# Fetching the value pages of a paged attention: 96 indirect DMAs on GpSimd instead of 384 register-addressed page loads

## The reference, cut to what matters

```python
gate = jnp.einsum('bqhd,bhnd->bqhn', qf, kmean)
...
top_s, top_i = lax.top_k(gate, K)
...
kg = kb[bi, hi, idx].astype(jnp.float32)
vg = vb[bi, hi, idx].astype(jnp.float32)
...
p = jax.nn.softmax(s.reshape(B, Q, H, -1), axis=-1).reshape(s.shape)
return jnp.einsum('bqhtk,bqhtkd->bqhd', p, vg)
```

## Time and profile before

| what | value |
|---|---|
| device time, median of 3 runs | 1584.08 us (1583.78 to 1584.59) |
| the profiled execution's own time | 1583.34 us |
| its span | 1581.5 us |
| PE busy | 1529.1 us, 97% |
| DVE, ACT, POOL busy | 944.3, 645.4, 186.9 us |
| DMA | 365.16 MB, mean 231 GB/s |

### The profile page before, as it was taken

One profiled execution on the slowest core, in us unless ns is written; L12 is line 12 of the kernel. 1 busy time (PEld: TensorE's weight loads), 2 busy tenths in 40 slices (PEclk: granted clock), 3 DMA queues, 4 the chain that ended last, 5 costly groups with the idle time before them and its releaser, 6 DMA issues.

```text
span 1581.5 us, 36029 instructions
## 1 busy us (share of the span) xinstructions
PE 1529.1 (97%) x14584; PEld 1484.6 (94%) x14584; DVE 944.3 (60%) x1159; ACT 645.4 (41%) x757; POOL 186.9 (12%) x287
## 2 busy tenths in 40 slices
PE   7999999999899889999999999999999999999996
PEld 7999999999798789998899999999999999999995
DVE  4445746567763355774586666666666644445566
ACT  5344343333424354464543433553333333333344
POOL 0000202021777300101000000000001000000000
PEclk9999999999999999999999999999999999999998
DMA  8788889785999975746644555556667655555453
GB/s 285 271 338 327 320 293 346 273 318 220 287 256 269 288 280 182 292 163 246 208 173 170 186 173 172 187 186 207 234 248 265 212 183 174 179 182 186 160 179 115
DMA packets 105635, 365.16 MB, mean 231 GB/s; under 512 B 14529, under 2 KB 48650, under 8 KB 78634
## 3 DMA queue, kind: packets, MB, share of 16 engines
q1 hardware_dynamic: 90834, 322.66, 58.8%
q0 software_dynamic: 12896, 39.73, 7.3%
q10 hardware_dynamic: 1792, 1.20, 0.4%
HBM read 353.27 MB, written 10.47 MB: 230 GB/s over the span
## 4 chain that ended last, share of the span: by engine, by line
PE 78%; DVE 7%; SPq 5%; ACT 4%; DMA 3%; issue 3%; ACTq 0%; DVEq 0%
PE psum_g L518 21%; PE psum_g L519 21%; PE psum_g L520 21%; PE M L2192 3%; PE M L2207 3%; DVE wl L502 2%; ACT wh L497 2%; SPq L612 2%; SPq L644 2%; PE M L518 1%; PE M L519 1%; PE M L520 1%; PE psum_g L2496 1%; SPq L684 1%; DMA raw<-w_in_t 1%
## 5 line engine op out<-in xcount | busy, mean ns | idle before, releaser
L518 PE MATMUL psum_g<-xh,wh 128*128 128x264 f32 (+1 forms) x2382 | 696.4, 292 | 7.3 <-DVE wl L502 3.7
L519 PE MATMUL psum_g<-xl,wh 128*128 128x264 f32 (+1 forms) x2382 | 677.5, 284 | 0.0
L520 PE MATMUL psum_g<-xh,wl 128*128 128x264 f32 (+1 forms) x2382 | 677.0, 284 | 0.0
L502 DVE TENSOR_TENSOR wl<-raw,wh 128x2048 fp32r<-128x2048 f32 (+1 forms) x205 | 462.9, 2258 | 305.1 <-ACT wh L497 304.2
L497 ACT CAST wh<-raw 128x2048 fp32r<-128x2048 f32 (+1 forms) x221 | 414.6, 1876 | 250.8 <-PE psum_g L520 205.0
L518 PEld LDWEIGHTS psum_g<-xh,wh 128*128 128x128 f32 x2382 | 450.5, 189 | 21.9 <-issue 14.9
L519 PEld LDWEIGHTS psum_g<-xl,wh 128*128 128x128 f32 x2382 | 450.8, 189 | 3.1 <-issue 2.9
L520 PEld LDWEIGHTS psum_g<-xh,wl 128*128 128x128 f32 x2382 | 448.8, 188 | 0.0
L518 PE MATMUL psum_g<-gh,wh 128*128 128x264 f32 x704 | 200.4, 285 | 0.3 <-DVE wl L502 0.3
L519 PE MATMUL psum_g<-gl,wh 128*128 128x264 f32 x704 | 199.4, 283 | 0.0
L520 PE MATMUL psum_g<-gh,wl 128*128 128x264 f32 x704 | 199.4, 283 | 0.0
(11 more groups left out here) (444 smaller groups left out, 1790.1 us busy)
## 6 DMA issues: line engine op xcount, KB each, us to landing
raw<-w_t SPq DMA_DIRECT2D x88, 1024.0 KB, 4.8
raw<-w_in_t SPq DMA_DIRECT2D x53, 1024.0 KB, 7.8
kring<-cache_k_t SPq DMA_DIRECT2D x96, 512.0 KB, 5.1
...
```

Of the source, the lines that this page charges most:

```text
L502: eng.tensor_tensor(wl[:, u % 2, 0:nk], raw[:, u % 2, 0:nk], wh[:, u % 2, 0:nk].bitcast(F32), ALU.subtract).then_inc(raw_used, 1)
L518: nc.tensor.matmul(out, hi_w, x_hi(k), start=(k == order[0]), stop=False)
L519: nc.tensor.matmul(out, hi_w, x_lo(k), start=False, stop=False)
L520: last = nc.tensor.matmul(out, lo_w, x_hi(k), start=False, stop=(k == order[-1]))
```

## The change

The values are laid out in DRAM as (page, head, token, dimension) and seen as rows of 2 KB, four tokens of one head; a page of one head is 32 such rows. An indirect DMA on POOL takes 128 row numbers from SBUF, one for each partition, and fetches 128 rows, so 4 pages: 256 KB. A group needs six. The row numbers are made on chip: DVE widens the six page numbers of each of 64 rows to 32 row numbers (`wide`), four small matmuls in unit 33 turn them onto 128 partitions, and DVE copies the 96 columns as integers (`v_index`). SP loads no pages any more. As each partition holds four tokens, the transposes of the probabilities become 16 matmuls with a column stride of 4, ACT copies the result in four pieces to two half-cleared rooms, and a group's matmuls take 16 columns of weights (two heads) instead of 8. POOL waits for the index before it does more, issues two groups, and `decays(3)` moves behind the second.

```diff
@@ -80,7 +80,7 @@
     part("eye8")[:] = np.eye(8).reshape(1, 64)
-    part("eye4")[:] = np.eye(4).reshape(1, 16)
+    part("v_row")[0:64] = 32 * (np.arange(64) % H)[:, None] + np.arange(32)[None]
     r = np.arange(P)
...
-        zp = zp_flat.rearrange("p (t h c) -> p t h c", t=2 * TOPK, h=H)
-        assert ATT + 1536 + ZP <= (K_RING - 2) * H * P
+        vk_rows = span(sraw, 3 * V_SLOT, 256).rearrange("p (w n) -> p w n", w=2)
+        ZP = H // 2 * 3 * 4 * 23
+        zp_flat = span(kring_flat, ATT + 1280, ZP)
+        zp = zp_flat.rearrange("p (r d e c) -> p r d e c", r=H // 2, d=3, e=4)
+        assert ATT + 1280 + ZP <= (K_RING - 2) * H * P
...
-        v_rooms = [(pj_flat, 8 * T), (pj_flat, 8 * T + V_SLOT), (pj_flat, 16 * T), (pj_flat, 16 * T + V_SLOT),
-                   (kring_flat, 0), (kring_flat, V_SLOT), (kring_flat, 2 * V_SLOT), (kring_flat, 3 * V_SLOT),
-                   (kring_flat, 4 * V_SLOT), (sraw, 0), (sraw, V_SLOT), (z_flat, 0)]
-        v_pages = [span(x, at_, V_SLOT).rearrange("p (t n) -> p t n", t=2 * TOPK) for x, at_ in v_rooms]
-        pid_row = C[0:1, _C["onehot_p"][0]:_C["onehot_p"][0] + 384].bitcast(I32)
+        v_rooms = [(pj_flat, (8 + 8 * n) * T + i * V_SLOT) for n in range(2) for i in range(3)]
+        v_rooms += [(kring_flat, i * V_SLOT) for i in range(7)]
+        v_rooms += [(sraw, i * V_SLOT) for i in range(3)] + [(z_flat, i * V_SLOT) for i in range(2)]
+        v_pages = [span(x, at_, V_SLOT) for x, at_ in v_rooms]
+        v_index = span(C, _C["onehot_p"][0], 96).bitcast(U32)
+        wide = span(C, _C["onehot_p"][0] + 96, 192, 64)
@@ -400,7 +400,7 @@
         slope_in = [sem(f"slope_in{s}") for s in range(2)]
-        v_full = [sem(f"v_full{s}") for s in range(12)]
+        v_full = [sem(f"v_full{s}") for s in range(6)]
         v_used, v_spread = sem("v_used"), sem("v_spread")
@@ -597,20 +597,17 @@
-        def load_values(eng, kind, group, heads):
+        def load_values(pool, group):
             b, half = divmod(group, 2)
-            at = (b * H + heads[0]) * 6
-            _, pages = nc.values_load_multi_w_load_instructions(
-                pid_row[:, at:at + 6 * len(heads)], engines={kind}, min_val=0, max_val=a["cache_v"].shape[1] - 1,
-                skip_runtime_bounds_check_because="each value is an entry of the page table")
             if group >= 3:
-                eng.wait_ge(v_used, group - 2)
-            for n_, h in enumerate(heads):
-                s = 4 * (group % 3) + h % 4
-                for t in range(6):
-                    eng.dma_start(v_pages[s][:, t], a["cache_v"][0, ds(pages[6 * n_ + t], 1), :, h].rearrange("a t d -> t (a d)"))\
-                       .then_inc(v_full[s], 16)
+                pool.wait_ge(v_used, group - 2)
+            for q in range(2):
+                for d in range(3):
+                    at = 32 * d + 4 * b + 2 * half + q
+                    pool.indirect_dma_start(v_pages[6 * (group % 3) + 3 * q + d], None, a["cache_v_t"],
+                                            bass.IndirectOffsetOnAxis(ap=v_index[:, at:at + 1], axis=0))\
+                        .then_inc(v_full[2 * (group % 3) + q], 16)
@@ -687,23 +680,8 @@
             ahead(35)
-            wait(sp, se_dve, "page_i")
-            sp.dma_start(pid_scratch, page_i[:, 0:6]).then_inc(d_pid, 16)
-            sp.wait_ge(d_pid, 16)
-            sp.dma_start(pid_row, pid_scratch.rearrange("r (a n) -> a (r n)", a=1)).then_inc(pid_back, 16)
-            sp.wait_ge(pid_back, 16)
-            values(0)
-            ahead(36)
-            values(1)
-            ahead(37)
-            wait(sp, e_dve, f"c{BLOCKS - 1}")
-            values(2)
-            ahead(38)
-            for group in range(3, 15, 2):
-                values(group)
-                values(group + 1)
-                ahead(39 + (group - 3) // 2)
-            values(15)
+            for u in range(36, 45):
+                ahead(u)
             wait(sp, b_dve, "ow", 3)
@@ -802,8 +780,8 @@
-            def values(group, heads=(2, 3)):
-                load_values(pool, mybir.EngineType.Pool, group, tuple(4 * (group % 2) + h for h in heads))
+            def values(group):
+                load_values(pool, group)
@@ -811,20 +789,22 @@
                 keep_edge(2 * p + 3)
-                store_state(p)
+                if p < 2:
+                    store_state(p)
+            wait(pool, e_dve, "index")
             pool.wait_ge(k_used, K_RING + NSAMP * PAGES)
+            values(0)
+            store_state(2)
+            nc.gpsimd.memset(pt_even[:, 128:256], 0.0)
+            nc.gpsimd.memset(pt_odd[:, 0:128], 0.0)
             nc.gpsimd.memset(zp_flat, 0.0).then_inc(e_pool.sem, 1)
+            values(1)
+            decays(3)
             pool.wait_ge(psum_free, 4 * turn + KEY_UNITS + 2)
             pool.dma_start(o["kv"][:, 0:8], kv[:, 0:8]).then_inc(e_out, 16)
-            pool.wait_ge(pid_back, 16)
-            values(0)
-            decays(3)
-            values(1)
             wait(pool, e_dve, f"c{BLOCKS - 1}")
-            values(2, (2,))
             wait(pool, e_pe, "pown")
-            values(2, (3,))
-            for group in range(3, 16):
+            for group in range(2, 16):
                 values(group)
@@ -1067,7 +1047,11 @@
                     wait(act, e_pe, "pown")
-                    nc.scalar.copy(pt.rearrange("p t n -> p (t n)"), M[:, 0, 0:384]).then_inc(e_act.sem, 1)
+                    wait(act, e_pool, "zp")
+                    nc.scalar.copy(pt_even[0:64], M[0:64, 0, 0:256])
+                    nc.scalar.copy(pt_even[64:P, 0:128], M[64:P, 0, 0:128])
+                    nc.scalar.copy(pt_odd[64:P], M[64:P, 0, 128:384])
+                    nc.scalar.copy(pt_odd[0:64, 128:256], M[0:64, 0, 256:384]).then_inc(e_act.sem, 1)
                 if 0 <= j - 1 < H:
@@ -1559,8 +1543,10 @@
                 wait(dve, se_dve, "page_f")
-                nc.vector.memset(page_i[:, 6:8], 0)
-                nc.vector.tensor_copy(page_i[:, 0:6], page_f[:, 0:6]).then_inc(se_dve.sem, 1)
+                nc.vector.scalar_tensor_tensor(wide.rearrange("p (s q) -> p s q", s=6),
+                                               page_f[:, 0:6].unsqueeze(2).to_broadcast([64, 6, 32]), 32.0 * H,
+                                               const("v_row", 64).unsqueeze(1).to_broadcast([64, 6, 32]), ALU.mult,
+                                               ALU.add).then_inc(se_dve.sem, 1)
@@ -1613,7 +1599,10 @@
                     wait(dve, e_act, "pt")
-                nc.vector.tensor_copy(zp[:, :, :, 7], pt[:, :, b * H:(b + 1) * H]).then_inc(v_spread, 1)
+                for d, room_, column in ((0, pt_even, 7), (1, pt_odd, 15)):
+                    ins = nc.vector.tensor_copy(zp[:, :, d:d + 2, :, column].rearrange("p r d e -> p r (d e)"),
+                                                room_.rearrange("p (x b r) -> p r x b", b=NSAMP, r=H // 2)[:, :, :, b])
+                ins.then_inc(v_spread, 1)
@@ -1728,7 +1721,10 @@
                     last_page()
-                    gather_blocks(0, 3)
+                    gather_blocks(0, 1)
+                    wait(dve, e_pe, "index")
+                    nc.vector.tensor_copy(v_index, M[:, 0, 0:96]).then_inc(e_dve.sem, 1)
+                    gather_blocks(1, 3)
                 elif u == KEY_UNITS + 1:
@@ -2312,14 +2308,18 @@
                     wait(pe, e_dve, "pown")
-                for g in range(4):
-                    pe.wait_ge(v_full[4 * (group % 3) + g], 96 * (group // 3 + 1))
+                for q in range(2):
+                    pe.wait_ge(v_full[2 * (group % 3) + q], 48 * (group // 3 + 1))
                 for t in range(6):
-                    for g in range(4):
-                        last = nc.tensor.matmul(M[32 * g:32 * g + 8, 0, half * P:(half + 1) * P],
-                                                zp[:, t, 4 * half + g, 7 - b:15 - b], v_pages[4 * (group % 3) + g][:, t],
-                                                start=(group == 0 and t == 0), stop=(group == 15 and t == 5),
-                                                skip_group_check=True)
+                    d, later = divmod(t, 2)
+                    for q in range(2):
+                        for x in range(2):
+                            rows, e_ = 32 * (2 * q + x), 2 * later + x
+                            last = nc.tensor.matmul(M[rows:rows + 16, 0, half * P:(half + 1) * P],
+                                                    zp[:, 2 * half + q, d, e_, 7 - b:23 - b],
+                                                    v_pages[6 * (group % 3) + 3 * q + d][:, e_ * P:(e_ + 1) * P],
+                                                    start=(group == 0 and t == 0), stop=(group == 15 and t == 5),
+                                                    skip_group_check=True)
                 last.then_inc(v_used, 1)
@@ -2349,17 +2349,23 @@
                     if u == KEY_UNITS + 1:
-                        wait(pe, e_dve, "prod")
```

(25 more changed lines are left out.)

47 lines of the change are left out of this document (22 added, 25 removed).

## The result

The changed kernel took **1590.99 us** (median of 20 runs, 1587.81 to 1596.87) against 1584.45 for the kernel before beside it (20 runs, 1578.28 to 1590.51). The ratio is 1.0040, with a 95% interval of 1.0028 to 1.0051: slower by 0.4%, where I had forecast 0.5% faster. Two later comparisons of the same two kernels gave more: 1.0188 (1.0168 to 1.0209) and 1.0174 (1.0158 to 1.0191). The experiments start from that difference.

A forecast was written before the change was run, and what follows sets the result against it. PE (97% busy), POOL's queue and the DMA engines were taken to run at nearly one rate. Gains of 7.3, 1.36 and 4.4 (13.1) less 4.8 give 8.3: 1584.08 to 1575.8 us, range 1568 to 1603.

The forecast's parts named there:

- Removed from SP: SP's queue loses 192 page loads, so weights issue earlier and PE's waits of 0.95 and 2.77 us go.
- L502's share of the 2.34: Masks on POOL no longer overlap DVE's L502 (3.65 against 2.29 us), saving 1.36 of PE's 2.34 us wait.
- DMA engines no bound: Larger pieces need about 278 GB/s where 357 had gone through; PE's page waits of 1.67 and 1.90 us go.
- PE, 16 matmuls at 0.22 each, +3.1: In unit 35, 16 matmuls at 0.22 us replace six transposes taking 0.4 us: 3.1 us added.
- POOL, order, "r up to 1.27 is free": Masks of pair 3 follow twelve gathers; up to 1.27 us a gather they would not delay PE.
- r: POOL's time for one gather in us, unknown beforehand and taken as 1.2.
- third rival: DVE's L502 holds gathers back, making 1.2 us a gather 1.39: 6.5 us lost, 1582.3 us; chance 7%.
- pown, and so the gathers' start, at 418.4: POOL waits for pown, at which ACT's L1070 starts; the last 84 gathers follow from 418.4 us.
- POOL, rate, "r <= 1.33": The last 84 gathers meet PE's need at group 15 if each takes at most 1.33 us; 1.2 leaves 10 us.
- first rival: POOL becomes the bound through gathers over 1.33 us, 1602.5 us at 1.6 us each; chance 28%.
- The clock, -4.4: Clock drops at 533 to 541 and 561 to 565 us vanish with the waits ahead of them: 2.7 and 1.7 us gained.

The follow-up runs named there:

- e3_again: Changed kernel with decays(3) ahead of the second gathers and probabilities sorted so the 16 matmuls read contiguous weights, run a second time: 1607.56 us, ratio 1.0141.
- the edited kernels: Changed kernel with masks ahead of the second six gathers, with sorted probabilities for contiguous weights, and with both: 1606.23, 1610.34 and 1605.04 us.
- h2_flip: Changed kernel with 48 added DVE instructions in units 37 to 42 that multiply the identity by the flip table, two different SBUF operands: 1611.06 us.
- f5_one: Changed kernel with 48 added DVE instructions in units 37 to 42 that multiply the identity by a constant: 1610.87 us.
- f2_spread_both: Changed kernel with each page group's matmuls issued four at a time, masks ahead of the second gathers and sorted probabilities: 1598.02 us, ratio 1.0073.

## Why the prediction was wrong

The forecast was 8.3 us faster; the first comparison measured 6.5 us slower. In its traced execution unit 35 lost 12.8 us and the other units from 33 to 45 won 5.8, so the steps that failed are those that lead into and follow from unit 35.

- **Removed from SP: right.** ACT's waits for weights went, PE's 2.77 became 0.26, and L502's share of the 2.34 became 1.00 (-1.34, forecast -1.36). That the tail would then be free was less sure than I wrote: the kernel before with only the order of tile 46 changed gained nothing (e4_before_tail).
- **DMA engines no bound: right** in the profile of after up to 533 (0.79 and 0.81, forecast under 0.9; 0.99 from 533 to 541). The stretched steps of later comparisons, some 17 to 27 us a run, are another matter. They make up the larger loss there (1.0188 and 1.0174), the forecast has no term and no rival for them, and of their cause it is shown only that a third fewer gathers take them away.
- **PE, 16 matmuls at 0.22 each, +3.1: the first step that failed.** They took 5.83 us, +5.2. The 0.22 held for contiguous weights (e3_again, 3.53 us in all); the stride of four elements was in the text but not in the price. The Trainium skill (SBUF — State Buffer, Door 1: The DMA port swizzle) says that SBUF has lines of 16 bytes and that each access that crosses to a new line costs extra, and four fp32 are 16 bytes. The trace agrees: 259 against 158 ns for the median weight load.
- **POOL, order, "r up to 1.27 is free": the second step that failed, and the costliest.** I put r = 1.2 over a margin of 0.07 and priced DVE's hold (third rival) at the average. An undisturbed gather took 1.25. In the first twelve, two were held by L502 (2.23 and 2.87 us) and others a little, so that they took (405.60 - 396.94) + (417.42 - 407.87) = 18.2 us, 1.52 each. The mask came 3.8 us later than at 1.2, straight onto PE, which lost 4.19. The bound itself was wrong too: it left out that PE gets there 1.36 us sooner, the gain at L502 that the same forecast counts. With it, 396 + 12r has to be at most 409.9, so r at most 1.16, and at 1.2 the mask was already half a us late. e1_masks shows the step as the cause: with the mask ahead of the second six gathers, unit 35 took 19.3 us, where the unedited kernel took 25.3 to 26.5.
- **pown, and so the gathers' start, at 418.4: failed with it.** In the profile's own time, 4.1 us late from before, that would be 422.5; it was 431.9. The mask wait (4.2), the longer matmuls (2.3 over the forecast) and the clock (3.3 up to there) add up to the delay, about. Four windows of the changed kernel:

```profile
416.00:420.00 4.00, 1.47 (x3) 0.83 (x3) 0.84 (x1) 2.82 (x3) 2.70 (x4) 0.54 0.98 363
420.00:424.00 4.00, 4.00 (x22) 3.60 (x21) 1.61 (x4) 0.00 (x0) 0.00 (x0) 0.61 0.58 243
...
428.00:432.00 4.00, 4.00 (x23) 3.72 (x23) 0.00 (x0) 0.85 (x3) 0.10 (x1) 0.74 0.01 4
432.00:436.00 4.00, 4.00 (x20) 4.00 (x20) 2.59 (x4) 2.02 (x8) 3.09 (x4) 0.50 0.38 129
```

Busy time by what the clock lacked is 1.47 x 0.46 + 4 x (0.39 + 0.26 + 0.50) = 5.3 us lost in unit 35. The first drop falls into the 4.19 us in which PE waited. The second comes while PE is fully busy, 4.00 of 4 us, with the narrow matmuls of L2385; no wait stands right before it.
- **POOL, rate, "r <= 1.33":** from 431.90 the last 84 gathers took (546.31 - 431.90) / 84 = 1.36 us each. With that rate and the late start, PE waited 1.83 + 3.27 + 2.86 us for the last groups. This is the first rival's mechanism: 7.96 us, where that rival had 26.7 for r = 1.6. (By the rival's own terms nothing of the 8.3 is left from r = 1.41, not 1.43.) No run shows what takes these waits away. Unit 43 fell from 17.9 to 10.9 us, without a page wait, in the edited kernels, but just so in the unedited one of the later comparisons, since PE was late there for its own reasons.
- **The clock, -4.4: gained and lost again.** The drops at 533 to 541 and 561 to 565 went (0.57 to 1.00 in both). Three others came: the two above, and one in 541 to 561 (0.91) behind the page wait of 2.86 us.
- **The Trainium skill's rule** (SBUF — State Buffer, Practical consequences), that DVE instructions with two SBUF inputs contend with a POOL instruction that reads SBUF, was the third rival at 7%. The trace agrees (13.5 us of stretches), and so does h2_flip with added instructions. It is not the whole: the TENSOR_SCALARs above held gathers too, f5_one's with a single SBUF input. The same page infers that descriptor making alone is not hit by them; the earlier trace rows agree for direct DMAs, so what waits is probably the reading of the row numbers. No run separates the two.

What remains open: why the first comparison's 20 runs (at most 1596.87 us, no stretched step in the one that was traced) and the later ones of the same kernel (at least 1610.75) differ. It goes with the occasion, and with how many landing records the traces have. The kernel before showed 1582.9 to 1585.8 as its median each time. No version of the gathers beat the kernel before with all its work. The nearest was the unedited one in the first comparison with 1.0040, and after it f2_spread_both with 1.0073.
